# Layer norms of a two-model transformer kernel: the eighth tile summed on VectorE, fewer means on TensorE, one low half on GpSimd

## What is computed

```python
def layer_norm(x, g, b):
    mu = jnp.mean(xf, axis=-1, keepdims=True)
    xc = xf - mu
    var = jnp.mean(xc * xc, axis=-1, keepdims=True)
    y = xc * lax.rsqrt(var + LN_EPS) * g.astype(jnp.float32) + b.astype(jnp.float32)
...
def first_block(...):
    for layer in range(DEPTH):
        x = layer_norm(DEEPNORM_ALPHA * x + 0.5 * swiglu(x, ...), ...)
        mix = rglru_block(x, ...) if layer < N_A else dilated_attention(x, k_shared, v_shared, ...)
        x = layer_norm(DEEPNORM_ALPHA * x + mix, ...)
        x = layer_norm(DEEPNORM_ALPHA * x + 0.5 * swiglu(x, ...), ...)
...
def second_block(x, meta, ...):
    h = layer_norm_2(jnp.concatenate([meta, x], axis=1), ...)
    for l in range(DEPTH):
        h = hybrid_layer(h, ...)      # two norms in each
    return h[:, N_META:]
```

## Time and profile before

| | us |
|---|---|
| median of 3 runs | 1757.0 |
| lowest, highest | 1755.71, 1757.52 |
| the profiled execution | 1757.72 |
| its span | 1755.9 |
| TensorE busy | 1723.1 |
| VectorE busy | 1241.3 |
| ScalarE busy | 972.5 |
| GpSimd busy | 0.2 |

### The profile page before, as it was taken

One profiled execution on the slowest core, in us unless ns is written; L12 is line 12 of the kernel. 1 busy time (PEld: TensorE's weight loads), 2 busy tenths in 40 slices (PEclk: granted clock), 3 DMA queues, 4 the chain that ended last, 5 costly groups with the idle time before them and its releaser, 6 DMA issues.

```text
span 1755.9 us, 33282 instructions
## 1 busy us (share of the span) xinstructions
PE 1723.1 (98%) x11772; PEld 1566.7 (89%) x11772; DVE 1241.3 (71%) x2175; ACT 972.5 (55%) x1700; POOL 0.2 (0%) x4
## 2 busy tenths in 40 slices
PE   8999998999999999999899999999999999999998
PEld 7888998888899888888788888989999999898887
DVE  6776789777664776677787766868665567787765
ACT  5564596655455655466565544565534346665543
POOL 0000000000000000000000000000000000000000
PEclk9999999999999999999999999999999999999999
DMA  6555355455544656533265563334455534345562
GB/s 225 191 201 194 132 181 181 143 186 200 192 142 157 202 186 218 162 116 123 87 217 191 184 213 133 101 117 132 148 175 188 184 114 132 115 145 191 191 203 85
DMA packets 76349, 288.80 MB, mean 164 GB/s; under 512 B 9312, under 2 KB 11616, under 8 KB 76256
## 3 DMA queue, kind: packets, MB, share of 16 engines
q1 hardware_dynamic: 76256, 287.53, 49.2%
HBM read 286.45 MB, written 1.05 MB: 164 GB/s over the span
## 4 chain that ended last, share of the span: by engine, by line
PE 92%; DVE 5%; ACT 2%; issue 1%; DMA 0%; SPq 0%; ACTq 0%; DVEq 0%
PE psum L526 33%; PE psum L527 17%; PE psum L518 12%; PE psum L520 11%; PE psum L519 11%; PE psum L657 1%; PE psum L769 1%; PE psum L604 1%; DVE wlo L1542 1%; PE psum L652 1%; DVE r_sq L1706 1%; ACT whi L1077 1%; PE psum L871 0%; DVE r_sq L1738 0%; PE psum L943 0%
## 5 line engine op out<-in xcount | busy, mean ns | idle before, releaser
L1542 DVE TENSOR_TENSOR wlo<-raw,whi 128x1024 fp32r<-128x1024 f32 (+2 forms) x494 | 640.7, 1305 | 281.2 <-ACT whi L1077 279.9
L526 PE MATMUL psum<-x_split,whi 128*128 128x512 f32 x1760 | 618.4, 395 | 4.3 <-DVE x_split L1577 3.1
L1077 ACT ACTIVATE whi<-raw 128x1024 fp32r<-128x1024 f32 (+2 forms) x494 | 544.8, 1116 | 37.8 <-PE psum L520 18.7
L527 PE MATMUL psum<-x_split,wlo 128*128 128x256 f32 x1760 | 494.5, 281 | 0.0
L526 PEld LDWEIGHTS psum<-x_split,whi 128*128 128x128 f32 x1760 | 331.5, 188 | 82.1 <-DVE x_split L1577 2.8
L518 PE MATMUL psum<-x_split,whi 128*128 128x272 f32 (+1 forms) x1168 | 342.1, 293 | 3.9 <-DVE x_split L1743 3.8
L520 PE MATMUL psum<-x_split,wlo 128*128 128x272 f32 (+1 forms) x1168 | 333.8, 286 | 0.0
L519 PE MATMUL psum<-x_split,whi 128*128 128x272 f32 (+1 forms) x1168 | 332.9, 285 | 0.0
L527 PEld LDWEIGHTS psum<-x_split,wlo 128*128 128x128 f32 x1760 | 331.8, 189 | 0.0
L526 PE MATMUL psum<-h_split,whi 128*128 128x512 f32 x770 | 272.2, 397 | 0.0
L518 PEld LDWEIGHTS psum<-x_split,whi 128*128 128x128 f32 x1168 | 220.2, 189 | 11.4 <-issue 6.3
(11 more groups left out here) (226 smaller groups left out, 1655.7 us busy)
## 6 DMA issues: line engine op xcount, KB each, us to landing
raw<-w_in SPq DMA_DIRECT2D x264, 512.0 KB, 3.3
raw<-w_out SPq DMA_DIRECT2D x96, 704.0 KB, 4.2
raw<-w_mix SPq DMA_DIRECT2D x42, 512.0 KB, 3.3
raw<-w_rg SPq DMA_DIRECT2D x25, 512.0 KB, 3.8
raw<-w_q SPq DMA_DIRECT2D x24, 512.0 KB, 3.3
raw<-w_kv SPq DMA_DIRECT2D x16, 512.0 KB, 3.3
raw<-w_mixo SPq DMA_DIRECT2D x16, 512.0 KB, 3.2
raw<-w_rg_out SPq DMA_DIRECT2D x8, 640.0 KB, 3.9
```

Source lines behind the costliest of these rows:

```text
L526: nc.tensor.matmul(ps[:, bank, :], whi[slot][:, w], split, start=start, stop=False)
L527: return nc.tensor.matmul(part(bank, 0), wlo[slot][:, w], split[:, 0], start=False, stop=stop)
L1077: nc.scalar.activation(whi[slot][:, 0:cols], raw[slot][:, 0:cols], ACT.Copy).then_inc(w_hi_done, count)
L1542: V.tensor_tensor(wlo[slot][:, 0:cols], raw[slot][:, 0:cols], f(whi[slot][:, 0:cols]), ALU.subtract).then_inc(w_lo_done, 1)
```

## The change

It touches ten of the eleven norms (all but `emb`), in five ways:

- VectorE adds the eighth tile to `sums` as well, values and squares apart, as two instructions behind the eighth tile. The semaphores `values_summed` and `squares_summed` replace `sums_done`.
- TensorE takes `means` and `token_means` of `sums` alone. The means of values stand in bank 2 and signal `value_means`; ScalarE's squared mean waits for that one and no longer for `stat_done`, for which VectorE's variance now waits. Seven keep-warm products stand ahead of the wait for the sum.
- The load of the root's table moves from `before_norm` to chunk `chunks - 4` of an `out` stage and to chunk 4 of the others.
- The low half of the next stage's third chunk is taken off VectorE; GpSimd has a program of its own for it, nine instructions in all.
- VectorE's low half of the fourth chunk, behind the norm, first waits until the third is done.

```diff
             else:
-                pe.wait_ge(sums_done, norm_stages.index(name) + 1)
-                means(sums[:, 0, :], first=True)
-                token_means(sums[:, 0, :], 0)
-                token_means(sums[:, 1, :], 4)
-
-                pe.wait_ge(acc_free, by_name[name].u0 + by_name[name].units)
-                means(r[:, KD - 1, :], last=True).then_inc(mean_done, 1)
-                token_means(r[:, KD - 1, :], 0)
-                pe.wait_ge(sq_done, KD * (n + 1))
-                ins = token_means(sq[:, KD - 1, :], 4, True)
+                ns = norm_stages.index(name)
+
+                pe.wait_ge(ax_shifted, (KD - 1) * (ns + 1))
+                keep_warm(7)
+                pe.wait_ge(values_summed, ns + 1)
+                means(sums[:, 0, :], True, True).then_inc(mean_done, 1)
+                token_means(sums[:, 0, :], 2).then_inc(value_means, 1)
+                pe.wait_ge(squares_summed, ns + 1)
+                ins = token_means(sums[:, 1, :], 5)
             ins.then_inc(stat_done, 1)
...
+    @block.gpsimd
+    def _(pool):
+        for name in norm_stages:
+            if by_name[name].next:
+                n, slot, _, cols = ahead(by_name[name].next, 0, 0)
+                pool.wait_ge(w_lo_done, n)
+                pool.wait_ge(w_hi_done, n + 1)
+                nc.gpsimd.tensor_tensor(wlo[slot][:, 0:cols], raw[slot][:, 0:cols], whi[slot][:, 0:cols].bitcast(fp32),
+                                        ALU.subtract).then_inc(w_lo_done, 1)
...
+        def root_table():
+
+            nc.scalar.activation(spare[:, :], eps[:, :], ACT.Sqrt)
+
         def before_norm(st):
 
-            nc.scalar.activation(spare[:, :], eps[:, :], ACT.Sqrt)
             if st.next:
                 round_chunk(*ahead(st.next, 0, 0))
...
             def out_step(i, j):
                 round_ahead(so, i, j)
+                if isinstance(i, int) and SLOTS * i + j == so.chunks - SLOTS:
+                    root_table()
...
                 round_ahead(st, i, j)
+                if m == SLOTS:
+                    root_table()
...
                 ns = norm_stages.index(name)
-                nc.scalar.activation(msq[:, 0:nt], ps[:, 5, 0:nt], ACT.Square).then_inc(msq_done, 1)
+                act.wait_ge(value_means, ns + 1)
+                nc.scalar.activation(msq[:, 0:nt], ps[:, 2, 0:nt], ACT.Square).then_inc(msq_done, 1)
                 act.wait_ge(var_ready, ns + 1)
...
-            if last and st.next:
-
-                rest_of_chunk(*ahead(st.next, 0, 0))
+            if last:
+
+                dve.wait_ge(acc_free, st.u0 + st.units)
+                V.tensor_tensor(sums[:, 0, t], sums[:, 0, t], r[:, m, t], ALU.add).then_inc(values_summed, 1)
+                dve.wait_ge(sq_done, KD * (norm_no[st.name] + 1))
+                V.tensor_tensor(sums[:, 1, t], sums[:, 1, t], sq[:, m, t], ALU.add).then_inc(squares_summed, 1)
...
                 dve.wait_ge(msq_done, ns + 1)
-                V.tensor_tensor(var_t[:, 0:nt], ps[:, 5, 4:4 + nt], msq[:, 0:nt], ALU.subtract).then_inc(var_ready, 1)
+                dve.wait_ge(stat_done, n + 1)
+                V.tensor_tensor(var_t[:, 0:nt], ps[:, 5, 0:nt], msq[:, 0:nt], ALU.subtract).then_inc(var_ready, 1)
...
                 if nxt:
+
+                    dve.wait_ge(w_lo_done, nxt.n0 + 3)
                     rest_of_chunk(*ahead(nxt, 0, 1))
```

More of the change, by code:

```diff
@@ L309, in build @@
     emb_squares = sem("emb_squares")
-    sums_done = sem("sums_done")
+    values_summed = sem("values_summed")
+    squares_summed = sem("squares_summed")
+    value_means = sem("value_means")
     stat_done = sem("stat_done")
@@ L648, in layer_norm, with token_means @@
             starts = token_starts(T)
-            started = []
             def means(tile, first=False, last=False):
                 return nc.tensor.matmul(acc(mean_bank(name), T), ones_d, tile[:, t], start=first, stop=last)
-            def token_means(tile, col, last=False):
+            def token_means(tile, bank, first=True, last=True):
                 for m, c in enumerate(starts):
-                    ins = nc.tensor.matmul(ps[:, 5, col + m:col + m + 1], tile[:, c:c + P], ones_d[:, 0:1],
-                                           start=not started, stop=last and m == len(starts) - 1, skip_group_check=True)
-                    started.append(1)
+                    ins = nc.tensor.matmul(ps[:, bank, m:m + 1], tile[:, c:c + P], ones_d[:, 0:1],
+                                           start=first and m == 0, stop=last and m == len(starts) - 1, skip_group_check=True)
                 return ins
@@ L669, in layer_norm @@
                     pe.wait_ge(sq_done, KD * n + k + 1)
-                    token_means(sq[:, k, :], 4)
+                    token_means(sq[:, k, :], 5, k == 0, False)
                 pe.wait_ge(emb_squares, 1)
-                ins = token_means(sums[:, 1, :], 4, True)
+                ins = token_means(sums[:, 1, :], 5, False)
             else:
-                pe.wait_ge(sums_done, norm_stages.index(name) + 1)
-                means(sums[:, 0, :], first=True)
-                token_means(sums[:, 0, :], 0)
-                token_means(sums[:, 1, :], 4)
-                pe.wait_ge(acc_free, by_name[name].u0 + by_name[name].units)
-                means(r[:, KD - 1, :], last=True).then_inc(mean_done, 1)
-                token_means(r[:, KD - 1, :], 0)
-                pe.wait_ge(sq_done, KD * (n + 1))
-                ins = token_means(sq[:, KD - 1, :], 4, True)
+                ns = norm_stages.index(name)
[6 more added lines that the diff above has]
+                ins = token_means(sums[:, 1, :], 5)
             ins.then_inc(stat_done, 1)
@@ L1208, in layer_norm @@
                     nc.scalar.activation(sq[:, k, :], r[:, k, :], ACT.Square).then_inc(sq_done, 1)
-            act.wait_ge(stat_done, n + 1)
             if name == "emb":
-                nc.scalar.activation(std_t[:, 0:nt], ps[:, 5, 4:4 + nt], ACT.Sqrt, bias=eps[:, 0:1]).then_inc(std_done, 1)
+                act.wait_ge(stat_done, n + 1)
+                nc.scalar.activation(std_t[:, 0:nt], ps[:, 5, 0:nt], ACT.Sqrt, bias=eps[:, 0:1]).then_inc(std_done, 1)
             else:
                 ns = norm_stages.index(name)
-                nc.scalar.activation(msq[:, 0:nt], ps[:, 5, 0:nt], ACT.Square).then_inc(msq_done, 1)
+                act.wait_ge(value_means, ns + 1)
+                nc.scalar.activation(msq[:, 0:nt], ps[:, 2, 0:nt], ACT.Square).then_inc(msq_done, 1)
                 act.wait_ge(var_ready, ns + 1)
@@ L1671, in add_tile @@
                 dve.wait_ge(sq_done, i + (KD * norm_no[st.name] + j))
-                ins = V.tensor_tensor(sums[:, :, t], sums[:, :, t], r_sq[:, :, i + (j - 1), t], ALU.add)
-                if last:
-                    ins.then_inc(sums_done, 1)
+                V.tensor_tensor(sums[:, :, t], sums[:, :, t], r_sq[:, :, i + (j - 1), t], ALU.add)
             dve.wait_ge(chunk_used, chunks_used)
```

## The result

The changed kernel takes 1760.65 us (median of 9 runs, 1759.71 to 1763.85); the kernel before took 1757.0 us beside it (9 runs). The ratio is 1.0025, with a 95% interval of 1.0016 to 1.0033. It is slower by a quarter of a percent. The forecast was 1751.8 us; the time is that of rival A (1760.4 us), which had a chance of 0.32.

What follows compares the result with a forecast made beforehand. TensorE, busy 98% of the span, was taken to bound the kernel, giving time back only around the norms. Gains of 1.6 + 3.4 + 1.0 = 6.0 us less 0.8 for GpSimd gave 5.2: 1757.0 to 1751.8 us, range 1750.2 to 1761.0.

Steps and rivals of the forecast that it cites:

- rival A: VectorE adds with two SBUF inputs stop fully while GpSimd works: 9.4 us lost in eight norms, 1760.4 us; chance 0.32.
- The adds and the means: Behind the eighth tile: adds 0.42 us, variance after 2.48 us (2.93 with 272 tokens); gains 1.6 and 3.4 us.
- the 6.0 us ahead of GpSimd's charge: Gain in ten norms before GpSimd's cost: 1.6 + 3.4 us from adds and means, 1.0 us from TensorE's clock.
- The clock: TensorE stays at the 2.4 GHz level from variance to scaling in o, mixo0 and out4; gain 1.0 us.
- The table load: Moved to an earlier step, its 1.28 us is covered by VectorE's idle time before the eighth tile; charged nothing.
- The low half on GpSimd: GpSimd's 2.4 us operation slows the add of values in rg_out, o, mixo0 and mixo1; 0.2 us each, 0.8 us.
- first sign: What would show rival A in the profile after: VectorE idle before the add of values; no size given.
- Rivals B and C: B: TensorE's clock still falls, 1753.8 us, chance 0.10; C: adds cost 0.69 us each, 1754.5 us, chance 0.08.

Runs made afterwards that it cites:

- e1: The changed kernel with one more wait: GpSimd takes the low half only after VectorE's two new adds; 1751.62 us against 1756.25, ratio 0.9974.
- e8: The kernel of e1 with the table load back in its old place, in before_norm; 1750.93 us against 1756.07, ratio 0.9969.
- e6: The changed kernel with GpSimd's subtraction replaced by a memset of 1408 columns, leaving out nine low halves; 1753.92 us in one execution.
- e7: The kernel of e1 without the seven keep-warm products ahead of the value sum; 1752.77 us against 1756.07, ratio 0.9983.

## Why the prediction was wrong

- **The adds and the means: right.** Expected 0.42 us for an add and the variance 2.48 us behind the eighth tile (2.93 with 272 tokens). Measured 0.42 to 0.43 us, 2.53 and 3.04 us, in e1 in every norm and in the changed kernel wherever GpSimd was done. Each variance is thus 0.05 to 0.1 us later than I had, 0.6 us in ten norms: of the 6.0 us ahead of GpSimd's charge e1 shows 5.4 us in the norms (56.0 - 50.6) and 4.6 us in the medians.
- **The clock: right with e1, wrong in the changed kernel.** With the adds on time, variance to scaling is 1.98 to 2.06 us in all ten norms of e1 (in e8 it was 2.10 us in `o`). In the changed kernel the longer wait let the clock fall in `o` (2.27 us) and the scaling of `mixo0` came late as before (2.44 us).
- **The table load: charged at nothing, and right as such** (e8); that it brings GpSimd to the seventh tile's add in `out0` to `out3` was said in rival A alone.
- **The low half on GpSimd: the step that failed.** "The bounds are 0 and a full stop of every add from two SBUF tensors", and of these I took 0.2 us in four norms, 0.8 us in all. The full stop is what happens. It costs the difference between the changed kernel and e1, 8.6 us in the norms where the sum had 0.8. It also reached `out0` to `out3`, which the sum left out: it named four norms, and eight lost time. The duration was right, 2.4 us taken and 2.39 measured. What I weighed wrongly was which end the price stands at: I put the value between free and an add twice as long, although the rule I cited said "the second to start stops until the first ends", and each of these adds met its condition. Every run here agrees with that rule of the Trainium skill (SBUF — State Buffer, Who interferes with whom), down to its exception: the eighth tile and the centring, with one SBUF input, were never held up, and neither was an add beside a GpSimd operation that only writes (e6). Twice VectorE's time for GpSimd, as the Trainium skill (GPSIMD Engine Reference, section 3) has it, is also what was measured: 2.39 against 1.2 us.
- **Rival A: the mechanism right, the parts less so.** It had 9.4 us of stops. Measured: the eighth tile starts 0.70 to 0.73 us after TensorE's last product in `out0` to `out3` against 0.32 before, about 0.4 late and not 0.75. GpSimd ended 0.23 us behind TensorE's last product, where rival A had 0.41 (the moved table load had brought VectorE's low halves and the seventh tile's add some 0.6 us later against that product, where I had 0.7 to 0.8); the held add ended 0.55 us behind GpSimd and not 0.69; and the eighth tile starts 0.08 us before that add ends. In `rg_out`, `o`, `mixo0` and `mixo1` the add of values was late by 0.73, 1.70, 1.30 and 1.42 us, where I had 1.0, 2.0, 1.6 and 1.75. That is 6.7 us in all. The rest of the 8.6 is TensorE's clock behind the longer waits: in `o` 1.2 us between the add and the variance and 0.3 us behind it, in `mixo0` 0.4 us behind it, which rival A left out. The two errors nearly cancelled, so that its 1760.4 us is closer to 1760.65 than its parts deserve. Its first sign, VectorE idle before the add of values, didn't come: the profile shows the stop as a longer add, not as idle time.
- **Rivals B and C** are not what made it slower: once the adds are on time the clock holds in e1 in all ten norms, and an add takes 0.42 us.

## What to carry to other kernels

Before work goes to GpSimd, list VectorE's operations that will run within its duration (here 2.4 us for 1024 columns) and count those with two SBUF inputs; each can lose nearly all that is left of GpSimd's instruction, and the one that stands on the critical path sets the price. A wait that holds GpSimd back until these are through costs nothing if its result is needed late: here it was worth 8 to 9 us. Where it can't be held back, cut its operation into pieces, which bounds a stop at one piece.

## What the runs showed of the hardware

- A VectorE add with two SBUF inputs and a GpSimd subtraction hold one another up, in both directions: an add of 0.69 us took 2.65 us behind GpSimd, and GpSimd took 2.89 us instead of 2.39 behind an add that had started 0.04 us before it.
- The stop is held for one instruction. Behind pieces of 256 columns the same add took 0.99 us; the pieces themselves had a mean of 880 ns with their own waits.
- A held add ended 0.29 us (0.42 us long) or 0.55 us (0.69 us long) after GpSimd's end, so by the profile about 0.13 us of its own time had passed while it was held, or GpSimd's reading ended that much before its recorded end; no run tells these apart.
- A GpSimd memset (1.27 us for 1408 columns) held up none of the nine VectorE adds that overlapped it.
- Beside GpSimd's subtraction VectorE's operations with one input in PSUM kept their time: 0.42 us for the eighth tile, 0.67 to 0.69 us for a centring of 512 columns.
- With seven products of 256 columns ahead of a wait, one every 0.12 us, TensorE stayed at the 2.4 GHz level through the norms of e1; in e7, without them, it fell in `o`. In e8, with them, it fell in `o` too, for about 3 us.
